# The output projection of a two-layer encoder as seven half-size products

## What is computed

```
m = sigmoid(gate_a) * (a @ w_branch_a) + sigmoid(gate_b) * (b @ w_branch_b)
x = x + rms_norm(m @ w_out, norm_mix_post)
f = conv_ffn(rms_norm(x, norm_ffn_pre), w_up, conv_w, conv_b, w_down)
x = x + rms_norm(f, norm_ffn_post)
```

## Time and profile before

| | us |
|---|---|
| median of three runs | 2427.83 |
| span of the profiled execution, first to last instruction | 2426.0 |
| TensorE busy | 2413.1 (99%) |
| VectorE busy | 1825.9 (75%) |
| ScalarE busy | 1302.4 (54%) |
| POOL busy | 195.1 (8%) |
| output projection of layer 0, first matmul to first of the up projection | 570.2 to 638.5 |

### The profile page before, as it was taken

The page is one execution under the profiler, slowest core; times in us unless marked ns, Lnnn a source line. Parts: engine busy times, 40 slices in busy tenths (PEclk is TensorE's granted clock), DMA queues, the critical chain, the costliest instruction groups (busy, mean ns, idle before and its releaser), DMA issues.

```text
span 2426.0 us, 40808 instructions
## 1 busy us (share of the span) xinstructions
PE 2413.1 (99%) x16410; PEld 2251.7 (93%) x16410; DVE 1825.9 (75%) x2403; ACT 1302.4 (54%) x2014; POOL 195.1 (8%) x236
## 2 busy tenths in 40 slices
PE   9999999999999999999999999999999999999998
PEld 9999989998999999888899998899989999998887
DVE  6666777754888998978585567777649889999784
ACT  6444666543555556556454456665436555554563
POOL 0001011100200000003110011011002000000031
PEclk9999999999999999999999999999999999999999
DMA  5454444344323233833233544343443232346421
GB/s 179 138 179 135 137 138 146 117 169 150 105 72 100 84 103 108 300 114 130 97 128 125 179 148 133 128 140 126 173 148 109 68 90 84 109 155 252 153 95 61
DMA packets 290411, 321.52 MB, mean 133 GB/s; under 512 B 10416, under 2 KB 223920, under 8 KB 290224
## 3 DMA queue, kind: packets, MB, share of 16 engines
q1 hardware_dynamic: 215744, 171.39, 22.7%
q10 hardware_dynamic: 74480, 147.53, 16.8%
HBM read 253.60 MB, written 65.27 MB: 131 GB/s over the span
## 4 chain that ended last, share of the span: by engine, by line
PE 96%; ACT 2%; issue 1%; DVE 1%; POOL 0%; ACTq 0%; DVEq 0%; POOLq 0%
PE ps L863 23%; PE ps L1143 14%; PE ps L1325 13%; PE ps L1088 9%; PE ps L836 6%; PE ps L1431 5%; PE ps L1071 5%; PE ps L1294 3%; PE ps L1261 3%; PE ps L850 3%; PE ps L1041 2%; PE ps L915 1%; PE ps L1411 1%; PE ps L1060 1%; PE ps L972 1%
## 5 line engine op out<-in xcount | busy, mean ns | idle before, releaser
L2048 DVE TENSOR_TENSOR wlo<-raw,whi 128x1024 fp32r<-128x1024 f32 (+1 forms) x152 | 163.9, 1079 | 54.8 <-ACT whi L3018 54.8
L863 PE MATMUL ps<-hT_hi,whi 128*128 128x384 f32 x608 | 203.1, 334 | 0.0
L863 PE MATMUL ps<-hT_hi,wlo 128*128 128x384 f32 x608 | 203.1, 334 | 0.0
L863 PE MATMUL ps<-hT_lo,whi 128*128 128x384 f32 x608 | 203.1, 334 | 0.0
L3032 ACT ACTIVATE U<-ps 128x384 f32<-128x384 f32 x152 | 74.8, 492 | 223.2 <-PE ps L863 223.2
L1325 PE MATMUL ps<-whi,PH_hi 128*128 128x512 f32 x456 | 179.0, 393 | 0.0
L1325 PE MATMUL ps<-whi,PH_lo 128*128 128x512 f32 x456 | 177.6, 390 | 0.0
L1325 PE MATMUL ps<-wlo,PH_hi 128*128 128x512 f32 x456 | 177.5, 389 | 0.0
L1509 DVE TENSOR_TENSOR wlo<-raw,whi 128x2048 fp32r<-128x2048 f32 x53 | 121.9, 2301 | 69.2 <-ACT whi L2368 69.2
L1637 DVE TENSOR_TENSOR wlo<-raw,whi 128x1024 fp32r<-128x1024 f32 (+1 forms) x98 | 102.8, 1069 | 79.3 <-ACT whi L2536 79.3
L863 PE MATMUL ps<-S_hi,whi 128*128 128x384 f32 x456 | 152.3, 334 | 0.0
(11 more groups left out here) (333 smaller groups left out, 6999.6 us busy)
## 6 DMA issues: line engine op xcount, KB each, us to landing
raw<-w_up_dram SPq DMA_DIRECT2D x88, 512.0 KB
raw<-w_in_dram SPq DMA_DIRECT2D x64, 512.0 KB
raw<-w_down_dram SPq DMA_DIRECT2D x60, 512.0 KB, 4.7
raw<-w_in_dram SPq DMA_DIRECT2D x16, 1024.0 KB
zT<-gst ACTq DMA_DIRECT2D x40, 384.0 KB, 2.4
GT<-zT ACTq DMA_DIRECT2D x16, 768.0 KB, 5.9
pD<-CG ACTq DMA_DIRECT2D x26, 384.0 KB, 2.3
zT<-hn ACTq DMA_DIRECT2D x48, 192.0 KB, 1.9
```

Source lines behind the costliest of these rows:

```text
L863: ins = mm(ps[:, 4 * (j % 2) + bank, 0:TH], quarter(L, W[y], j, (w,))[:, 0, k * P:(k + 1) * P], sum_operand(a, x, k), start=(opens and k = ...
L2048: v.tensor_tensor(lo, x, hi.bitcast(F32), ALU.subtract)\
```

## The change

The product is computed in Strassen's form with seven products and shared sums. The 768 tokens and the 1024 rows and columns of `w_out` are each cut in two halves: tokens 0-383 (three tiles) and 384-767; B11, B12, B21, B22 are quarters of `w_out`, 4 k-rows by 512 columns. With T1 = B12 - B11, T2 = B22 - T1, T3 = T2 - B11, N4 = T2 - B21, and token sums S1, S2, S4 of `m` (R1, R2, R4 in float32; `WSUM` in two parts), the products run in the order P2, P1, P5, P6, P3, P7, P4, each whole over three token tiles, each tile 4 k x 3 passes of 128x512. P2 runs with k outside. P2 and P5 open banks 0 to 2 and P1 banks 3 to 5; P6 and P7 add to P1's banks, P3 to P5's, and P4 to P7's. Copies C11, C12, C22 take what is shared (ScalarE: `s2`, `s5`, `u2`; VectorE adds: `c11`, `c12`, `c22`).

- `w_out`: B21 and B11 are loaded as units; B12 and B22 go as whole float32 quarters into the memory of X (`EA`, tiles 4 and 5; `EB`, tiles 2 and 3), which is free then. VectorE forms the T sums in `EA` and `raw`. All six further products are split into `whi` and `wlo` in the two slots.
- SP's queue now loads X in three pairs, each after what lay in its place is used; the first two up units are held until N4 and P7's low part are done.
- The branch stage forms R1, R2, R4 with further subtractions of 384 tokens, and on ScalarE a copy for the first four blocks.
- `JK`, ScalarE's scratch for squares, moves to the memory of `gst1`, inside R4; the rows `wrows` lie inside R1 and R2 and are loaded later.
- `TMP` is now the memory of `hn`. The slots and semaphore counts of all later units are renumbered (36 instead of 32 for the first up unit); their order stays.

The core of the diff (indentation cut, empty lines left out; helpers `out_weight_high`, `out_weight_low` and `out_sum_low` are one copy or one subtraction each, `out_chunk` is the three matmuls of one tile and k):

```diff
-    for i in range(2):
-        for u in range(2):
-            load(unit(L, U_WO + u, i), [rows(w_out, L, 4 * u, 4, i * 512, 512)])
-    for j in range(NFF):
-        load(unit(L, U_UP + j), [rows(w_up, L, 0, KD, j * P + half, P) for half in (0, FF)])
+    sp.wait_ge(ab_dve.sem, ab_dve.at(L, f"l{KD - 1}"))
+    for i, (dst, k0) in enumerate(((EA, 0), (EB, 4))):
+        sp.dma_start(dst.rearrange("p (k n) -> p k n", n=512), rows(w_out, L, k0, 4, 512, 512)).then_inc(wo_ld[i], 16)
+    sp.wait_ge(s_out, L * 192 + 16)
+    residual_rows(L, 0)
+    load(unit(L, U_WO), [rows(w_out, L, 4, 4, 0, 512)])
+    load(unit(L, U_WO + 1), [rows(w_out, L, 0, 4, 0, 512)])
+    def up_rows(j):
+        return [rows(w_up, L, 0, KD, j * P + half, P) for half in (0, FF)]
+    sp.wait_ge(wo_sum.sem, wo_sum.at(L, "N4"))
+    load(unit(L, U_UP), up_rows(0), held=wo_product(L, "P1"))
+    sp.wait_ge(w_lo, wo_product(L, "P3")[0] + (1 + CREDIT))
+    residual_rows(L, 1)
+    load(unit(L, U_UP + 1), up_rows(1), held=wo_product(L, "P7"))
+    sp.wait_ge(w_lo, unit(L, U_WO + 7)[0] + (1 + CREDIT))
+    residual_rows(L, 2)
+    for j in range(2, NFF):
+        load(unit(L, U_UP + j), up_rows(j))
     for r in range(PIECES):
         if r < 4:
...
+    def out_tile(name, t):
         if t == 0:
-            unit_ready(w)
+            unit_ready(unit(L, U_WO + 7) if name == "P4" else wo_product(L, name))
+        if name in A_SUM_OF and t == 0:
+            pe.wait_ge(wo_dve.sem, wo_dve.at(L, A_SUM_OF[name]))
+        if name == "P1":
+            pe.wait_ge(br_dve.sem, br_at(L, 7 if t else 6, "tb"))
+        elif name in ("P5", "P3", "P7"):
+            pe.wait_ge(wo_act.sem, wo_act.at(L, f"{({'P5': 's2', 'P3': 's5', 'P7': 'u2'}[name])}_{t}"))
+        else:
+            pe.wait_ge(wo_dve.sem, wo_dve.at(L, f"{({'P6': 'c11', 'P4': 'c22'}[name])}_{t}"))
         for k in range(4):
-            for q, (a, b) in enumerate(PASSES):
-                ins = mm(ps[:, t, :], mT[a][:, 4 * u + k, t * P:(t + 1) * P], W[b][:, w[3], k * 512:(k + 1) * 512],
-                         start=(u == 0 and k == 0 and q == 0), stop=(u == 1 and k == 3 and q == 2))
-        if t == NT - 1:
+            ins = out_chunk(name, t, k)
+        if wo_counted(name, t):
             ins.then_inc(w_used, 1)
-        elif u:
-            ins.then_inc(*wo_pe.step(f"a1_{t}"))
+        else:
+            ins.then_inc(*wo_pe.step(f"{name}_{t}"))
+    unit_ready(unit(L, U_WO))
+    pe.wait_ge(br_dve.sem, br_at(L, 6, "tb"))
+    for k in range(4):
+        pe.wait_ge(br_dve.sem, br_at(L, 4 + k, "ml"))
+        for t in range(HT):
+            ins = out_chunk("P2", t, k)
+            if k == 3 and t < HT - 1:
+                ins.then_inc(*wo_pe.step(f"P2_{t}"))
...
+    for what, n in (*WO_TILES[HT:-4], (TURN, 0), ("P7", 2), ("P4", 0), (TURN, 1), ("P4", 1), (TURN, 2), ("P4", 2),
+                    (UP, 0), (TURN, 3), (UP, 1), (TURN, 4), (UP, 2), (TURN, 5), *((UP, n) for n in range(3, 8))):
...
+            first, second = (C11[:, r, :], C12[:, r, :]) if r < HT else (ps[:, r, :], C22[:, r - HT, :])
+            for src, c0, k in ((first, 0, "ra"), (second, 512, "rb")):
+                v.scalar_tensor_tensor(TMP[:, c0:c0 + 512], src, rsy[:, r:r + 1], wrows[:, 1, c0:c0 + 512], ALU.mult, ALU.mult)\
+                    .then_inc(*c["dve"].step(f"{k}{r}"))
             done(c["dve"], it, f"rb{r}")
+            if r % 2 == 0:
...
+                if i == 0:
+                    v.tensor_tensor(R1[:, q, :], BT1[:, TH:T], BT2[:, TH:T], ALU.add).then_inc(*br_dve.step(f"r{q}"))
+                    v.tensor_tensor(BT1[:, 0:TH], BT1[:, 0:TH], BT2[:, 0:TH], ALU.add).then_inc(*br_dve.step(f"m{q}"))
+                    done(br_dve, L, f"m{q}")
+                    v.tensor_tensor(BT1[:, TH:T], BT1[:, 0:TH], R1[:, q, :], ALU.subtract).then_inc(*br_dve.step(f"s{q}"))
+                else:
+                    v.tensor_tensor(BT1[:], BT1[:], BT2[:], ALU.add).then_inc(*br_dve.step(f"m{q}"))
+                    done(br_dve, L, f"m{q}")
+                    v.tensor_tensor(R1[:, q - 4, :], R1[:, q - 4, :], BT1[:, TH:T], ALU.add).then_inc(*br_dve.step(f"r{q}"))
+                done(br_act, L, f"mh{q}")
+                v.tensor_tensor(mT_lo[:, q, :], BT1[:], mT_hi[:, q, :].bitcast(F32), ALU.subtract).then_inc(*br_dve.step(f"ml{q}"))
+                if i:
+                    v.tensor_tensor(R2[:, q - 4, :], BT1[:, TH:T], R2[:, q - 4, :], ALU.subtract).then_inc(*br_dve.step(f"s{q}"))
+                    done(br_dve, L, f"s{q}")
+                    v.tensor_tensor(R4[:, q - 4, :], BT1[:, 0:TH], R2[:, q - 4, :], ALU.subtract).then_inc(*br_dve.step(f"p{q}"))
...
+    def out_weight_sum(name):
+        if name == "T1":
+            dve.wait_ge(wo_ld[0], L * 16 + 16)
+            _, half, s, _ = unit(L, U_WO + 1)
+            dve.wait_ge(w_loaded[s], half * 32 + 32)
+        elif name == "T2":
+            dve.wait_ge(wo_ld[1], L * 16 + 16)
+            dve.wait_ge(w_lo, wo_product(L, "P5")[0] + (1 + CREDIT))
+        elif name == "T3":
+            dve.wait_ge(w_lo, wo_product(L, "P6")[0] + (1 + CREDIT))
+        else:
+            done(wo_sum, L, "T3")
+        out_, x, y = {"T1": (EA, EA, raw[:, 1, :]), "T2": (EA, EB, EA), "T3": (raw[:, 1, :], EA, raw[:, 1, :]),
+                      "N4": (EA, raw[:, 0, :], EA)}[name]
+        v.tensor_tensor(out_, x, y, ALU.subtract).then_inc(*wo_sum.step(name))
...
+    out_weight_sum("T1")
     low(unit(L, U_WO + 1))
-    low(unit(L, U_WO + 2))
-    for t in range(NT):
-        done(wo_act, L, f"sq{t}")
-        v.tensor_copy(Y0w[:, t, :], ps[:, t, :]).then_inc(*wo_dve.step(f"y{t}"))
-    low(unit(L, U_WO + 3))
+    out_sum_low("S1", R1)
+    out_weight_low("P5", EA)
+    out_weight_sum("T2")
+    out_sum_low("S2", R2)
+    for t in range(HT):
+        out_sum("c11", t)
+    out_weight_low("P6", EA)
+    out_weight_sum("T3")
+    out_weight_sum("N4")
+    out_sum_low("S4", R4)
+    out_weight_low("P3", EB)
     dve.wait_ge(s_wr, L * 80 + 48)
-    done(wo_dve, L, f"y{NT - 1}")
-    for n in range(3):
-        dve.wait_ge(s_x[n], L * 16 + 16)
+    def row_sums(s):
+        for name, t in ((("c12", 0), ("c12", 1)), (("c12", 2),), (("c22", 0),), (("c22", 1), ("c22", 2)))[s] if s < 4 else ():
+            if (name, t) == ("c12", 1):
+                out_weight_low("P7", raw[:, 1, :])
+            if (name, t) == ("c22", 0):
+                last_weight_low()
+            out_sum(name, t)
     def turned_sums(t):
         for name in ("S1", "S2", "S3"):
             sum_turned(L, name, t)
-    norm_stage(nr, L, X, Y0w, lambda t: None, lambda s: low(unit(L, U_UP)) if s == 3 else None,
+    norm_stage(nr, L, X, row_sums, lambda s: low(unit(L, U_UP)) if s == 3 else None,
...
+                done(br_dve, L, f"{'m' if i else 's'}{q}")
+                a(mT_hi[:, q, :], BT1[:], ACT.Copy).then_inc(*br_act.step(f"mh{q}"))
+                if i == 0:
+                    a(R2[:, q, :], BT1[:, TH:T], ACT.Copy).then_inc(*br_act.step(f"cr{q}"))
...
+    def out_square(t):
+        if t < HT:
+            done(wo_dve, L, "S4" if t == 0 else f"c11_{t}")
+            src = C11[:, t, :]
+        else:
+            done(wo_dve, L, f"c22_{t - HT}")
+            src = C22[:, t - HT, :]
+        if t:
+            done(*((wo_act, L, f"sq{t - 1}") if t < HT else (nr["act"], L, f"sqy{t - 1}")))
...
     high(unit(L, U_WO + 1))
-    high(unit(L, U_WO + 2))
-    for t in range(NT):
-        if t < NT - 1:
-            done(wo_pe, L, f"a0_{t}")
-        else:
-            used(unit(L, U_WO + 1))
-        if t == 0:
-            done(br_dve, L * 2 + 1, "ml1_1")
-        else:
-            done(wo_act, L, f"sq{t - 1}")
-        a(JK[:], ps[:, t, :], ACT.Square, scale=1.0 / 32, accum_out=ssy[:, t:t + 1]).then_inc(*wo_act.step(f"sq{t}"))
-    high(unit(L, U_WO + 3))
+    act.wait_ge(br_dve.sem, br_at(L, KD - 1, "p"))
+    out_sum_high("S1", R1)
+    for t in range(HT):
+        out_copy("s2", t)
+    done(wo_sum, L, "T1")
+    out_weight_high("P5", EA)
+    out_sum_high("S2", R2)
+    out_sum_high("S4", R4)
+    done(wo_sum, L, "T2")
+    out_weight_high("P6", EA)
+    done(wo_dve, L, "S2")
+    row(wrows[:, 0, :], n_ffn_pre, L, s_wr)
+    row(wrows[:, 1, :], n_mix_post, L, s_wr)
+    for t in range(HT):
+        out_square(t)
+    for t in range(HT):
+        out_copy("s5", t)
+    act.wait_ge(wo_ld[1], L * 16 + 16)
+    out_weight_high("P3", EB)
+    out_copy("u2", 0)
+    out_copy("u2", 1)
     def wo_bank(t):
-        if t == 0:
-            done(wo_act, L, f"sq{NT - 1}")
-        if t < NT - 1:
-            done(wo_pe, L, f"a1_{t}")
-        else:
-            used(unit(L, U_WO + 3))
+        if t == 1:
+            out_copy("u2", 2)
+            done(wo_sum, L, "T3")
+            out_weight_high("P7", raw[:, 1, :])
+        if t == 2:
+            done(wo_sum, L, "N4")
+            n, _, _, g = wo_product(L, "P4")
+            act.wait_ge(w_used, n + 1)
+            for i in range(2):
```

(48 more changed lines are left out.)

148 lines of the change are left out of this document (81 added, 67 removed).

## The result

The changed kernel takes 2440.1 us, the median of 4 runs (2438.72 to 2443.25), against 2427.80 for the kernel before on the same chip. The ratio is 1.0052, with a 95% interval of 1.0038 to 1.0066: half a per cent slower. The profiled execution took 2438.72 with a span of 2436.6 us, 10.6 more than before; the forecast was 10.0 more.

A forecast was written before the change was run, and what follows sets the result against it. TensorE was taken to bound the kernel. Per layer -8.2 for matmuls, +2.3 +2.8 +0.9 for P1, P3, P7, +6.3 normalization, +0.9 after: +5.0; 2426.0 + 2 x 5.0 + 1.8 = 2437.8 us, own range 2433 to 2444, with rivals 2425 to 2447.

The forecast's parts named there:

- Saving: Output projection: 252 matmuls instead of 288, 8.2 us a layer less, 16.3 in all.
- P1: Before product P1, TensorE waits 2.3 us for its wlo, because T1 stands ahead of it on VectorE.
- P3: Before product P3, TensorE waits 2.8 us for its wlo, at 608.0, behind S4's low part and ScalarE's squares and copies.
- P7: Before product P7, TensorE waits 0.9 us; its whi stands on ScalarE behind C12's first square, wlo at 617.2.
- The stretch from 617: Normalization: 25.3 us of VectorE work against TensorE's 19.0; up projection starts at 642.5, 4.0 us late; +6.3 with restarts.
- the walk: Following the engines' queues in order with layer 0's times, to find each wait; it gave +5.0 us a layer.
- After it: After the up projection starts: last tile's low part 5.1 us later, half a us of slack used up; +0.9, TensorE 5.0 late.
- POOL beside VectorE: POOL contends with two-input VectorE instructions, so rsy and rsx come later: 0 to 1 us a layer more.
- (a): VectorE keeps pace in the projection and most of the saving stays: 2418 us, or 2411.5 without P1's and P7's waits; chance 0.12.
- (b): Stretch from 617 is 4 to 5 us shorter by earlier HN tiles, so both come out even: 2427 to 2429, chance 0.06.
- (d): A late transfer, of EA or X's pairs, holds VectorE 3 us or more: 2443 to 2450, chance 0.06.
- rival (c): TensorE's clock falls after the three waits over 2 us, 7 us a layer longer: 2452, chance 0.08.

The follow-up runs named there:

- the second experiment on the order: The changed kernel with the low part of S4 made directly behind P6's, ahead of T3 and N4: 2435.36 us, ratio 1.0033.
- The two fillers: The changed kernel with two unused 128x1024 VectorE subtractions, behind S4's low part (2443.52 us) or behind the sum of C12's second tile (2447.43 us).
- three orders changed: The changed kernel with P1's wlo ahead of T1, S4's low part directly behind P6's, and P7's split directly behind P3's: 2424.70 us, ratio 0.9988.
- with less work besides: Three-orders kernel with C11 premultiplied by norm weights and shorter residuals for tiles 0 to 2 (2421.73 us), then C12's first sum ahead of P7's low part: 2421.03 us.
- after: The changed kernel itself, against the kernel before: 2440.1 us, ratio 1.0052.
- the fillers at 617: The changed kernel with two unused 128x1024 VectorE subtractions behind the sum of C12's second tile: 2447.43 us, ratio 1.0081.

## Why the prediction held, point by point

- **Saving.** 8.2 us a layer was right: 16.0 measured for both.
- **P1.** 2.3 forecast; measured 2.05 in the bracket, 2.3 with what a wait costs beside it. T1 ahead of the wlo is shown as the cause by turning the two about: that wait went. What this saves is seen only with the next cause gone too, and there only as a difference.
- **P3.** 2.8 forecast; 2.37 in the bracket, some 2.6 with the rest. The chain (S4's low part behind T3 and N4, then squares, copies, whi, wlo) was right link by link: the first square at 599.57 for 599.7, the wlo at 605.22 + 2.29 = 607.5 for 608.0. Shown by the second experiment on the order.
- **P7.** 0.9 forecast; 0.77 in the bracket, some 1.0 with the rest.
- **The stretch from 617.** The first up part starts at 642.37, the walk had 642.5. The two fillers show that VectorE is the bound there and not at 599. VectorE "without a gap" was wrong by one: 0.44 us before the first HN, where POOL's rsx came late. The prediction had named such a gap as a sign against the walk, and it is a small one. It did not make that HN late: P7's low part ended at 616.74 and not at 617.2, and this head start was used up by the 0.44, so HN ended at 623.55 + 1.28 = 624.83 for 624.9. TensorE, with P7 begun 0.4 us earlier too, so waited 2.35 for it and not 2.0.
- **After it.** The size was right and the step was not, so the 5.0 is in part luck. The walk let the last tile's low part be the one that TensorE waits for, with the half us between them used up. It ends at 661.92 + 0.68 = 662.60 against 657.46, 5.14 later for 5.1; but TensorE wants it after one up part begun at 659.07, at 663.3, so the half us is still there. What TensorE waited for came earlier: the fourth HN (0.45 before 647.24) and the low part of the second up unit (0.37 before 653.77), which ended at 651.43 + 2.28 = 653.71. These made it 5.15 late for 5.0. VectorE's own delay grew there by two idle times for POOL. Before the fifth row it is 1.03 against 0.85 before, 0.18 more where 0.45 was added for ScalarE's further square. Before the sixth it is 0.46, where the walk had none, after POOL steps of 1.34 and 1.45 us.
- **POOL beside VectorE.** The rule of the Trainium skill on shared interfaces (GPSIMD Engine Reference, Specifications) was weighed at 0 to 1 us a layer. The two idle times that the walk did not have, 0.44 and 0.46, lie in that. The POOL steps ahead of both stand in the chain that ended last, at 621.30 and 644.74.
- **Rivals.** (a), that VectorE keeps pace and most of the saving stays, did not occur, and in no order that was tried: with three orders changed 3.1 of the 16 us are kept, with less work besides 6.7, and with the three orders VectorE is still busy 24.12 of the 25 us from 611 to 636. (b) and (d) did not occur; no row of TensorE or VectorE in this stretch of the trace waits for a transfer.
- **The clock, rival (c).** I put it at 7 us a layer with a chance of 0.08. It is neither absent nor that large. In after's profiled execution the clock reads 1.00 after waits of 2.05, 2.37 and 2.35 us; in the other three its mean was 0.999, 0.998 and 0.996 and they took 2439.34, 2440.85 and 2443.25. The median is so 1.4 us above the profiled execution. Of the 2.3 us by which the forecast was short, 1.4 are this, 0.6 are span, and 0.3 are the distance between time and span, 2.1 us in place of 1.8. That the 1.4 are the clock's goes with the mean clocks and is not shown, since these executions have no trace. TensorE: Matmul & The Clock Gate of the Trainium skill, Why this matters for your kernels, says that an idle TensorE falls back to half rate; the runs agree, 0.50 granted behind 4.03 us.

## What to carry to other kernels

A saving on the bound engine is kept only if the work that it adds elsewhere is done when that engine asks for it, so add up the other engine's work from the last idle time before the demand, not over the stage. When both helpers show long idle times ahead of a late one (here 5.68 and 8.68 us before a wait of 2.37), look for a chain between them: a scratch tile placed in someone's memory, or a step queued behind sums that nobody needs yet. Order those queues by due time before judging the idea: the same algorithm was 12.3 us slower than the kernel before, or 3.1 us faster with three queues reordered, and 6.7 us faster with some work moved out of the busy stretch as well, its products and their order unchanged.

## What the runs showed of the hardware

- A wait of 2.5 us of TensorE, between two stretches in which it was busy, costs about 4.1 us: behind it matmuls of 128x512 start 0.43 us apart in place of 0.23 for 3.0 to 3.4 us. A wait of 1.2 us costs 1.2 to 1.4. A wait of 2.04 us before P1 did it in layer 0 and not in layer 1 of one execution (the fillers at 617), and waits of 2.05 to 2.37 did not in after's profiled one. That after's runs spread over 4.5 us, with mean clocks of 0.999 to 0.996, goes with it; which waits did it in the other three has no trace.
- The fall need not come with the wait: behind 2.49 us the first matmuls still started 0.34 and then four times 0.23 to 0.26 apart, and then the clock fell. In layer 1 of the same execution it fell within 0.9 us of the restart. A slow stretch should be looked for a few us behind the idle time too.
- As in the earlier trace rows, a POOL step of one column took 2.34 us beside VectorE's HN and the subtraction behind it, and another such step 0.19 a little later, in the kernel after:
```profile
623.71 2.34 POOL L2437 TENSOR_SCALAR msy<-ssy 128x1 f32<-128x1 f32 x1 [0.20 <-ACT JK L2545]
...
627.61 0.19 POOL L2428 TENSOR_SCALAR msx<-ssx 128x1 f32<-128x1 f32 x1
```
